# A hybrid encoder step on one core: 24 of attention's weight tiles split and stored during the pooling stages, and the stores of the middle activations moved one unit back

## The reference

```python
x = x + gate * pool_mixer(rms_norm(x) * (1 + scale) + shift)     # layer 0
x = x + gate * attention(rms_norm(x) * (1 + scale) + shift)      # layer 1
y = rms_norm(x)
# pool_mixer: u, g = h @ w_in; trailing means of u over 2, 4, 8, 16 rows minus u;
#   a 256x256 product in each of 4 groups; times silu(g); @ w_out
# attention: q, k, v, g = h @ w_in; 16 heads, 4 key/value heads, a window of 128 earlier rows
#   in chunks of 64, ALiBi, a sink per head; times silu(g); @ w_out
# shift, scale, gate = silu(c) @ ada_w[layer] + ada_b[layer], for the prompt and for the sample
```

## Time and profile before

| | |
|---|---|
| median of three runs | 1714.47 us (1714.03 to 1714.68) |
| the profiled execution | 1710.07 us |
| its span, first to last instruction | 1708.1 us |
| mean granted TensorE clock | 0.964 |
| PE busy | 1595.4 us, 93% of the span |
| weight loads into PE (PEld), DVE, ACT, POOL busy | 80%, 51%, 44%, 25% |
| DMA | 316.90 MB, 186 GB/s over the span |

### The profile page before, as it was taken

The page is one execution under the profiler, slowest core; times in us unless marked ns, Lnnn a source line. Parts: engine busy times, 40 slices in busy tenths (PEclk is TensorE's granted clock), DMA queues, the critical chain, the costliest instruction groups (busy, mean ns, idle before and its releaser), DMA issues.

```text
span 1708.1 us, 27931 instructions
## 1 busy us (share of the span) xinstructions
PE 1595.4 (93%) x9083; PEld 1361.7 (80%) x9083; DVE 866.5 (51%) x2194; ACT 747.4 (44%) x1658; POOL 420.2 (25%) x403
## 2 busy tenths in 40 slices
PE   5899999999999999988888899999999999999998
PEld 3789987777777777788877788888788887888876
DVE  2555434433442444246666534677436765367751
ACT  3434332223222322246565543665545665456552
POOL 0333420011001100234434541233312333122331
PEclk8899999999999999999889889999999999999998
DMA  7777686556656655563434445433454334553323
GB/s 271 281 256 257 231 293 231 211 211 228 234 191 246 210 206 184 214 227 127 146 114 149 173 148 201 162 135 124 173 189 157 124 139 147 210 175 125 125 72 126
DMA packets 167605, 316.90 MB, mean 186 GB/s; under 512 B 21359, under 2 KB 88255, under 8 KB 167214
## 3 DMA queue, kind: packets, MB, share of 16 engines
q1 hardware_dynamic: 167470, 315.12, 52.7%
HBM read 240.96 MB, written 74.31 MB: 185 GB/s over the span
## 4 chain that ended last, share of the span: by engine, by line
PE 80%; DVE 6%; issue 4%; ACT 4%; DMA 1%; POOL 1%; SPq 0%; DVEq 0%; POOLq 0%; ACTq 0%
PE ps_u L832 65%; PE ps_o L1060 3%; PE ps_t L1033 3%; PE ps_s L1014 2%; PE ps_s L1015 2%; PE ps_s L863 1%; DMA work<-in_x_prompt_dram 1%; ACT work L1634 1%; DVE ps_u L1215 1%; ACT ps_u L1529 1%; PE ps_t L1073 1%; DVE ps_o L1393 1%; POOL work L1768 1%; DVE acc L1407 1%; PE ps_o L875 1%
## 5 line engine op out<-in xcount | busy, mean ns | idle before, releaser
L832 PE MATMUL ps_u<-h_all_hi,w_hi 128*128 128x512 f32 (+2 forms) x1440 | 525.2, 365 | 11.3 <-DVE acc L1224 6.3
L832 PE MATMUL ps_u<-h_all_lo,w_hi 128*128 128x512 f32 (+2 forms) x1440 | 515.6, 358 | 0.0
L832 PE MATMUL ps_u<-h_all_hi,w_lo 128*128 128x512 f32 (+2 forms) x1440 | 515.1, 358 | 0.0
L832 PEld LDWEIGHTS ps_u<-h_all_hi,w_hi 128*128 128x128 f32 x1440 | 279.8, 194 | 64.8 <-issue 17.8
L832 PEld LDWEIGHTS ps_u<-h_all_hi,w_lo 128*128 128x128 f32 x1440 | 278.9, 194 | 36.2
L832 PEld LDWEIGHTS ps_u<-h_all_lo,w_hi 128*128 128x128 f32 x1440 | 279.4, 194 | 34.4
L832 PE MATMUL ps_u<-y_hi,w_hi 128*128 128x512 f32 (+1 forms) x640 | 236.1, 369 | 12.8 <-POOL y_lo L1747 6.9
L832 PE MATMUL ps_u<-y_hi,w_lo 128*128 128x512 f32 (+1 forms) x640 | 230.3, 360 | 0.0
L832 PE MATMUL ps_u<-y_lo,w_hi 128*128 128x512 f32 (+1 forms) x640 | 230.1, 360 | 0.0
L1215 DVE TENSOR_TENSOR ps_u<-ps_u,rstd_b 128x512 f32<-128x512 f32 (+1 forms) x180 | 107.1, 595 | 208.1 <-PE ps_u L832 200.9
L1768 POOL TENSOR_TENSOR work<-work,recip 128x512 f32<-128x512 f32 (+2 forms) x136 | 132.9, 998 | 256.5 <-DVE recip L1380 256.5
(11 more groups left out here) (197 smaller groups left out, 2268.9 us busy)
## 6 DMA issues: line engine op xcount, KB each, us to landing
w_hi<-w_hi_kept SPq DMA_DIRECT2D x156, 512.0 KB, 3.6
w_lo<-w_lo_kept SPq DMA_DIRECT2D x156, 512.0 KB, 4.5
w_hi_kept<-w_hi SPq DMA_DIRECT2D x52, 512.0 KB, 2.7
w_lo_kept<-w_lo SPq DMA_DIRECT2D x52, 512.0 KB, 4.3
chunks<-in_ada_w_dram SPq DMA_DIRECT2D x32, 512.0 KB, 5.7
w_raw<-in_pool_w_in_dram SPq DMA_DIRECT2D x16, 512.0 KB, 5.6
w_raw<-in_attn_w_in_dram SPq DMA_DIRECT2D x16, 512.0 KB, 4.9
work<-in_x_prompt_dram SPq DMA_DIRECT2D x12, 512.0 KB, 6.0
```

The costliest lines, as they stand in the source:

```text
L832: last = nc.tensor.matmul(out, w, x, start=(i == 0), stop=(i == n - 1))
```

## The change

Two things are changed in the step list, and the engines follow.

1. The first 24 home tiles of attention (all 20 of its input projection and 4 of the 8 output tiles) are `fore` tiles. They are no longer loaded raw and split in the ring. In pooling stages 1 to 3, eight in each, SP loads them raw into two buffers of their own (FL), ACT and POOL split them there (FW), and SP stores both halves (FS). In stage 4 they are fetched, as in all later stages. FW of a tile stands behind the first u unit of a group, or behind the first gate unit, on ACT and POOL; FS and the FL of the tile two further stand behind the second u or gate unit. That FL waits for the stores of its buffer, issued just ahead of it, to have landed. The buffers lie in SBUF that attention uses later, so `CHUNKS` falls from 4 to 3, `kv_t` and `kv_keep` change places, and the first writers of attention wait for the last stores (`fore_done`).
2. `out_units` appends XM of a block behind the evacuation of the block after it, also among the first three units. In parts 1 to 3, XM of block 0 stood ahead of all output units; now it stands behind the evacuation of the second. From block 2 on the order is as before.

```diff
-CHUNKS = 4
+CHUNKS = 3
+FORE = 2
+EARLY = 24
...
+        self.fore = [names[t][0] for t in self.tiles[PARTS * len(names) // 2:]][:EARLY]
...
-        self.steps = [s for s in self.steps if s[0] != "W" or (s[1] < len(self.tiles) and self.home[s[1]] == s[1])]
+        self.steps = [s for s in self.steps if s[0] != "W" or (s[1] < len(self.tiles) and self.home[s[1]] == s[1] and s[1] not in self.fore)]
...
+    def early(self, p, n):
+        if p:
+            i = EARLY // 3 * (p - 1) + n
+            self.steps.append(("FW", i))
+
+    def early_out(self, p, n):
+        if p:
+            i = EARLY // 3 * (p - 1) + n
+            self.steps.append(("FS", i))
+            if i + FORE < EARLY:
+                self.steps.append(("FL", i + FORE))
...
+        if p == 1:
+            for i in range(FORE):
+                s.append(("FL", i))
         for g in range(GROUPS):
             for i in range(2):
                 emit(self.group(p, self.tile(("pin", 2 * g + i)), "u", n=2 * g + i, g=g, i=i))
+                if i == 0:
+                    self.early(p, 2 * g)
+                else:
+                    self.early_out(p, 2 * g)
                 if g < 2:
                     self.ada(1)
...
+                if i == 1:
+                    self.early_out(p, 2 * g + 1)
                 if i == 0:
+                    self.early(p, 2 * g + 1)
                     s.extend(late + [("PQ", p, g, 1)])
...
+        def finish(u, k_from=0):
+            self.project(u, k_from)
+            s.append(("E1", u))
+            if layer == 0 and self.units[u]["b"] == len(self.blocks(p)) - 1:
+                if made:
+                    s.append(("XM", p, made[-1]))
+                made.append(self.units[u]["n"])
...
                 for i in range(3):
-                    self.project(order[i], done[i])
-                    s.append(("E1", order[i]))
+                    finish(order[i], done[i])
                     self.split_to(j + AHEAD)
             for u in fresh:
-                self.project(u)
-                s.append(("E1", u))
-            if layer == 0 and n:
-                s.append(("XM", p, n - 1))
+                finish(u)
...
+                elif st[0] == "FL":
+                    i = st[1]
+                    if i >= FORE:
+                        sp.wait_ge(fore_kept[i % FORE], 32 * (i // FORE))
+                    else:
+                        sp.wait_ge(dve_const, 2)
+                    load_raw(tiles[fore[i]], fore_raw[:, i % FORE, :], fore_loaded[i % FORE])
+                elif st[0] == "FS":
+                    i = st[1]
+                    sp.wait_ge(fore_hi_ready, i + 1)
+                    sp.wait_ge(fore_lo_ready, i + 1)
+                    at = kept.index(fore[i])
+                    sp.dma_start(w_hi_dram[at], fore_hi[:, i % FORE, :].bitcast(F32)).then_inc(fore_kept[i % FORE], 16)
+                    sp.dma_start(w_lo_dram[at], fore_raw[:, i % FORE, :]).then_inc(fore_kept[i % FORE], 16)
...
+                elif kind == "FW":
+                    i = st[1]
+                    act.wait_ge(fore_loaded[i % FORE], sum(32 if tiles[fore[n]][0] == "kv" else 16 for n in range(i + 1) if n % FORE == i % FORE))
+                    A(fore_hi[:, i % FORE, :], fore_raw[:, i % FORE, :], ACT.Copy).then_inc(fore_hi_ready, 1)
...
+                elif kind == "FW":
+                    i = st[1]
+                    pool.wait_ge(fore_hi_ready, i + 1)
...
+                    raw = fore_raw[:, i % FORE, :]
+                    G.tensor_tensor(raw.bitcast(F32R), raw, fore_hi[:, i % FORE, :].bitcast(F32), ALU.subtract).then_inc(fore_lo_ready, 1)
```

More of the change, by code:

```diff
@@ L271, in out_units @@
         s = self.steps
-        order = []
+        order, made = [], []
+        def finish(u, k_from=0):
[5 more added lines that the diff above has]
+                made.append(self.units[u]["n"])
         for n in range(KT):
@@ L414, in trunk_kernel @@
         q_st = sb("q_st", [P, 4, COLS], F32R)
-        kv_t = sb("kv_t", [P, WINDOW + COLS])
         with nc.sbuf_tensor("chunks", [P, CHUNKS, 1024], F32) as chunks:
-            pass
+            with nc.sbuf_tensor("fore_raw", [P, FORE, 1024], F32) as fore_raw, nc.sbuf_tensor("fore_hi", [P, FORE, 1024], F32R) as fore_hi:
+                pass
         pt_hi, pt_lo = sb("pt_hi", [P, 1024], F32R), sb("pt_lo", [P, 1024], F32R)
@@ L478, in trunk_kernel @@
         ada_loaded = [sem(f"ada_loaded{i}") for i in range(LANDING + CHUNKS)]
+        fore_loaded, fore_kept = [sem(f"fore_loaded{i}") for i in range(FORE)], [sem(f"fore_kept{i}") for i in range(FORE)]
+        fore_hi_ready, fore_lo_ready = sem("fore_hi_ready"), sem("fore_lo_ready")
         mid_stored, mid_loaded = [sem("mid_stored0"), sem("mid_stored1")], sem("mid_loaded")
@@ L519, in own, with fore_done @@
         def own(j):
-            return home[j] == j
+            return home[j] == j and j not in fore
         def splits(j):
-            return sum(1 for i in kept if i <= j)
+            return sum(1 for i in kept if i <= j and own(i))
         def keeps(j):
-            return sum(1 for i in kept if i <= j and i % RING == j % RING)
+            return sum(1 for i in kept if i <= j and i % RING == j % RING and own(i))
+        def fore_done(eng):
+            for i in range(FORE):
+                eng.wait_ge(fore_kept[i], 32 * sum(1 for n in range(EARLY) if n % FORE == i))
+            eng.wait_ge(ada_done, KT * len(sched.mods))
         def fetches(j):
@@ L662, in _, with load_raw @@
         def _(sp):
[L663 to L671, removed]
+            def load_raw(t, slot, s):
+                dst = slot.rearrange("p (k n) -> p k n", k=KT)
                 if t[0] == "pin":
@@ L687, in load_tile @@
                                      src[:, :, at + 64 * t[1]:at + 64 * t[1] + 64]).then_inc(s, 16)
+            def load_tile(j):
+                t = tiles[j]
+                if j >= RING:
+                    tile_used(sp, j - RING)
+                    if own(j - RING):
+                        sp.wait_ge(w_kept[j % RING], 32 * keeps(j - RING))
+                load_raw(t, w_raw[:, j % RING, :], raw_loaded[j % RING])
             def keep_tile(j):
@@ L1306, in _ @@
                     else:
-                        dve.wait_ge(ada_done, KT * len(sched.mods))
+                        fore_done(dve)
                     if p:
@@ L1513, in _ @@
                                 act.wait_ge(k_prev, n)
+                            elif u["b"] == 0:
+                                fore_done(act)
                         if k == "u" and u["b"] == 0:
@@ L1694, in _ @@
                                     w_hi[:, j % RING, 0:width[j]].bitcast(F32), ALU.subtract).then_inc(w_lo_ready, 1)
+                elif kind == "FW":
+                    i = st[1]
+                    pool.wait_ge(fore_hi_ready, i + 1)
+                    pool.wait_ge(fore_loaded[i % FORE], sum(32 if tiles[fore[n]][0] == "kv" else 16 for n in range(i + 1) if n % FORE == i % FORE))
+                    raw = fore_raw[:, i % FORE, :]
+                    G.tensor_tensor(raw.bitcast(F32R), raw, fore_hi[:, i % FORE, :].bitcast(F32), ALU.subtract).then_inc(fore_lo_ready, 1)
                 elif kind == "NA":
```

15 lines of the change are left out of this document (9 added, 6 removed).

## The result

| | before | after |
|---|---|---|
| median of four runs each, same chip | 1714.25 us (1711.94 to 1714.68) | 1697.37 us (1694.5 to 1701.54) |
| profiled execution, its span | 1710.07, 1708.1 us | 1699.7, 1697.9 us |
| mean granted clock | 0.964 | 0.967 |

The ratio is 0.9906 (0.988 to 0.9932): faster by 16.9 us, 1.0%, where 41 us were forecast. One run of experiment 5 further down took 2314 us at a granted clock of 0.62 and is left out of its median. First the page of the changed kernel: POOL's work has not shrunk, the 24 subtractions stand in another place.

What follows compares the result with a forecast made beforehand. The prediction took PE as the bound (busy 93%), losing time in attention of part 0 to a chain of dependent steps and a lower clock. Gains 22 + 9 + 10.4 = 41.4 us, 1714.5 - 41.4 = 1673 us; range 1646 to 1700.

Steps and rivals of the forecast that it cites:

- 4. SP's queue: Pooling stages: FL's 24 waits for just-issued stores, 4.3 us each, leave fetches 8 us of 17.6 us slack; cost 0.
- Step 5: Pooling-stage traffic: 1.5 MB per moved tile raises the DMA share from 0.62 to about 0.84; cost 0.
- The slower rival: Pooling stages: FL's wait holds fetches, PE waits 2.5 us per tile, 19 us slower, 1733 us; chance 5%.
- The rival of 1697 us: Attention of part 0: DVE's order takes over, freed time is waited for elsewhere, only 7 + 10.4 us come; chance 22%.
- Splits out of attention: Attention of part 0: 24 ACT copies and 24 POOL subtractions leave; 22 us of waits and 9 of clock.
- The term for the maximum: Attention of part 0: two small steps behind the maximum shorten, 4.7 us, plus 1.05 in the drain, together 5.7.
- Step 1: Attention of part 0, splits removed: PE's waits shrink for SR by 13.3, gating 2.9, maximum 5.7; sum 22 us.
- POOL's place in the queue: Attention of part 0: waits directly behind subtractions in POOL's queue, 2.9 + 4.3 = 7 us, the lower bound of the waits.
- the exclusion: Attention of part 0: DVE steps held by SBUF-reading POOL instructions; SR's sum 6.1 us, v split 2.9, small steps 4.7.
- XM: 10.4 forecast: Output part of pooling stages 1 to 3: loads of x go out some 14 us earlier, gaining 2.3, 3.3 and 4.8 us.
- Splits in the pooling stages, chunks and traffic: Pooling stages: added splits covered by 2.4 us of slack, ada_w chunks landing in time, extra bytes harmless; each cost 0.
- The lock rival: Pooling gate half, 12 groups: POOL's subtraction holds scan and low half, 2.4 us each, 29 in all, 1702 us; chance 6%.

Runs made afterwards that it cites:

- experiment 5: experiment 3 plus, at 21 old split places in attention of part 0, an ACT copy and a POOL subtraction of 128x1024 on unused data: 1702.30 us.
- experiment 3: The changed kernel with each FL one step later, ahead of the next FW, so the stores it waits for are older: 1674.07 us, ratio 0.9777.
- experiment 9: experiment 3 with the second FW of each group put ahead of the pooled row's own steps: 1674.64 us, ratio 0.9777.
- experiments 7: experiment 3 plus ACT's copy alone at 21 old split places in attention of part 0, nothing added on POOL: 1688.63 us, ratio 0.9854.

## Why the prediction was wrong

**The step that failed is "4. SP's queue", priced at 0.** It reckoned 17.6 us from one issue to the need, less "block 4.3, landing taken alike, about 1 for the issues". Measured were a block of about 9.6 us (77 in 8), a landing of 7.5 for a fetch, and 1 for the issues: 18.1, and the slack of 8 us is gone. (There are 22 such waits, not 24: the first two tiles find free buffers.) The 4.3 of the earlier trace rows is a median of 4.6 us in pooling stage 0, at a DMA share of 0.76, and 4.0 in attention of part 0 at 0.46, where a pair of stores goes out ahead of the next loads and not behind fetches. Step 5 worked out the new share, 0.84, nearly rightly (0.82 measured), and I did not carry it back into step 4. The share alone would not have done it: with the landings of experiment 3, 7.6 us for the store and 6.3 for a fetch at a share of 0.89, the same sum leaves 17.6 - 7.6 - 6.3 - 1 = 2.7 us, an estimate. What step 4 did not see is that the wait makes its own bursts, in which the stores that it waits for come last. The loss is 20 us by stages (498.8 against the 479.1 of experiment 3) and 23 by medians. Of the 20, 6 stand in PE's busy time (484.1 against 478.2 us, at clock 0.99 against 1.00), and 14 in the profile as PE's waits between 242 and 735 us:

```profile
PE ps_u L894 <- issue: 8.1, 6, 2.4
PE ps_s L925 <- DMA chunks<-in_ada_w_dram: 3.9, 3, 1.5
PE ps_s L950 <- DMA work<-in_x_prompt_dram: 1.9, 1, 1.9
```

PE's first group is marked "issue"; I take it for a wait for fetched weights, and it is gone in experiment 3. I had named such waits as what would prove me wrong. The slower rival had the mechanism and an outsized price: 23 us over 24 early tiles is about 1 us a tile, not 2.5, and not enough to eat the gain. The rival of 1697 us hit the number by luck and for a wrong reason, since DVE's order did not take over: attention of part 0 gained 25.7 us. The range of 1646 to 1700 took in the measured 1697.37 us only by that rival; the forecast itself, 1673 us and 41 us of gain, was missed by 24 us, and its own range of 1660 to 1687 by 10.

**The other steps, with the queue out of the way (experiment 3, 1674.07), come to about 39 us, where 41.4 were forecast. That is in part luck, as the errors of the terms cancel.**

- *Splits out of attention: 31 forecast, 25.7 measured.* Period 54.5 us against about 54 forecast, clock 0.94 against 0.93. The 22 us of waits were 12.7: SR's fell by 10.2 (13.3 forecast), the gating's by 8.8 (2.9), the maximum's by 2.2 (5.7), and 8.5 came back in the wait ahead of PV, which I had not foreseen. The term for the maximum took it that both small steps behind it would be free of POOL, and the first still stands beside `y_lo`. Step 1 also followed PE's waits one by one, and not the chain over ACT and DVE up to PV, whose 5.0 us stayed while PE's unit beside it became 1.5 us shorter. PE's busy time, though, fell by 13 us, where 9 were put down to the clock. The sum, 26 for 31, was nearer than any of its terms.
- *Who caused it* was further off. POOL's place in the queue, the part I thought safest at 7 us, is worth about 0.5, and the exclusion, 6.1 + 2.9 + 4.7 = 13.7 in the sum, 11.7. ACT's copies got 1.05 us in the drain, and are worth 13.5, probably since they stand ahead of the exponentials and evacuations that feed the chain (that they cost this is shown, the path by which is not). I had looked for POOL in the waits, as PE named it, and not at what ACT does ahead of it.
- *XM: 10.4 forecast,* 12.1 alone and 13.3 with FL later by the medians, 12.7 and 12.2 by the stages.
- *Splits in the pooling stages, chunks and traffic: 0 forecast,* about 1 us all together by stages. The lock rival was given 29 us as its price; experiment 9, built to bring it about, held the low half but never the scan, and cost nothing beyond the spread of the runs.
- *The profiled execution.* Its span fell by 10.2 us only: it is 2.3 us above its median and that of before 4.2 below its own. Its opening and pooling stage 0 are 7.3 us longer than before, and no other kernel here shows as much (stage 0 took 173.6 to 176.3 in them, with three chunks alone 175.6, and the two together were at most 4.2 us longer than before). What made them so in this one execution is open.

## What to carry to other kernels

A queue that issues a store and then waits for it to land stops everything behind it, and the burst that follows makes the next store slower. Put the step that needs the store one or two steps on, where it is old; and take the landing time behind what the queue will have issued just ahead of it and at the DMA share that the change will bring, not as the trace of before has it. To price work that leaves an engine, ask who stands behind it on that engine, ACT as well as the one that PE's wait names, and put dummy work of the same size back to see which part of it counted. Follow the whole chain that PE waits for, since a wait taken away at one link can come back at the next.

## What was not expected of the hardware

- Stores of 512 KB took 9.4 and 10.3 us (median of high and of low halves) to land at a DMA share of 0.82 in bursts, and 6.7 and 7.6 us at 0.89 when spread out; in pooling stage 0 before, 3.3 and 4.6 us at 0.76. Between the first two the order of the issues mattered more than the load.
- With each microsecond of PE's wait taken out of attention, PE's busy time fell by about another: 12.7 and 13.3 us in the change, at clock 0.90 and then 0.94, and 7 and 7 between experiments 7 and 3, at 0.93 and 0.94.
- Two memsets of 1.91 us on POOL in place of a subtraction of 2.38 us cost the stage 0.5 us, and the subtraction 12.2, both over ACT's copies alone.
